# One token block's gate cells: scattered by accumulating indirect transfers in place of one-hot products

## The reference, cut to what matters

```
q = h @ w_q                                    # 8 heads, two halves of 128
s1, s2 = q_half @ sub_keys_{1,2}.T             # 128 scores each
v1, i1 = top_k(s1, 16);  v2, i2 = top_k(s2, 16)
best, ci = top_k(v1[:, None] + v2[None, :], 16)   # 16 pairs of 256, per head
expert = i1[ci // 16] * 128 + i2[ci % 16]
gate = softmax(best)
a = gelu(h . U[expert]) * gate                 # 128 experts a token
out = sum over the 128 of a * V[expert]
```

## Time and profile before

| | |
|---|---|
| median of 3 runs | 2063.12 us (2060.56 to 2063.41) |
| the profiled execution | 2064.9 us, of which the span is 2063.1 us |
| TensorE busy | 2032.0 us, 98% |
| VectorE busy | 1641.9 us, 80% |
| ScalarE busy | 893.3 us, 43% |
| GpSimd busy | 383.9 us, 19% |
| moved by DMA | 471.40 MB, 228 GB/s over the span |

### The profile page before, as it was taken

One profiled execution on the slowest core, in us unless ns is written; L12 is line 12 of the kernel. 1 busy time (PEld: TensorE's weight loads), 2 busy tenths in 40 slices (PEclk: granted clock), 3 DMA queues, 4 the chain that ended last, 5 costly groups with the idle time before them and its releaser, 6 DMA issues.

```text
span 2063.1 us, 28548 instructions
## 1 busy us (share of the span) xinstructions
PE 2032.0 (98%) x10753; PEld 1763.9 (85%) x10753; DVE 1641.9 (80%) x3092; ACT 893.3 (43%) x1369; POOL 383.9 (19%) x297
## 2 busy tenths in 40 slices
PE   8999999999999999999999999999999999999998
PEld 6877788887887788889999999999998888888886
DVE  5787567666986545899999999888668888888887
ACT  5566454544245423534344444444334333333334
POOL 2000110000000001000221222222223444444440
PEclk9999989999999999999999999999999999999999
DMA  7511145531221132224879989999999999999993
GB/s 252 174 51 43 51 161 192 183 143 62 92 82 72 62 102 87 80 82 136 273 263 306 343 285 333 341 319 347 360 355 402 359 376 372 376 370 369 373 375 137
DMA packets 136856, 471.40 MB, mean 228 GB/s; under 512 B 10048, under 2 KB 59456, under 8 KB 110992
## 3 DMA queue, kind: packets, MB, share of 16 engines
q1 hardware_dynamic: 49936, 309.33, 41.2%
q0 software_dynamic: 36864, 134.23, 16.7%
q10 hardware_dynamic: 49920, 26.01, 4.3%
HBM read 416.97 MB, written 52.43 MB: 228 GB/s over the span
## 4 chain that ended last, share of the span: by engine, by line
PE 39%; DVE 10%; issue 1%; ACT 0%
PE bank L158 38%; DVE whl L311 2%; DVE row L2332 2%; DVE room L2276 1%; DVE fg L2283 1%; DVE room L2272 0%; DVE room L2200 0%; DVE cst L2200 0%; DVE y_tok L2200 0%; DVE room L2204 0%; DVE y_tok L2204 0%; DVE cst L2204 0%; DVE cidx L1988 0%; DVE wk L1982 0%; DVE cidx L1980 0%
## 5 line engine op out<-in xcount | busy, mean ns | idle before, releaser
L158 PE MATMUL bank<-xhl,whl 128*128 128x384 f32 (+1 forms) x5256 | 1073.4, 361 | 16.1 <-DVE whl L543 8.2
L158 PEld LDWEIGHTS bank<-xhl,whl 128*128 128x128 f32 x5256 | 935.7, 188 | 103.1 <-issue 10.2
L311 DVE TENSOR_TENSOR whl<-raw,whl 128x1024 fp32r<-128x1024 f32 (+2 forms) x397 | 472.6, 1201 | 198.9 <-ACT whl L304 152.5
L158 PE MATMUL bank<-whl,ag 128*128 128x512 f32 x2304 | 526.3, 390 | 0.8 <-issue 0.8
L158 PEld LDWEIGHTS bank<-whl,ag 128*128 128x128 f32 x2304 | 431.4, 188 | 91.5 <-ACT whl L304 2.0
L304 ACT ACTIVATE whl<-raw 128x1024 fp32r<-128x1024 f32 (+2 forms) x397 | 398.8, 1024 | 86.7 <-PE bank L158 78.6
L2319 POOL DMA_INDIRECT row<-in_U_rows,row_at x128 | 149.5, 1168 | 597.9 <-DVE row L2332 429.8
L2319 POOL DMA_INDIRECT row<-in_V_rows,row_at x128 | 191.0, 1492 | 251.3 <-DVE y_tok L2348 221.8
L2348 DVE SCALAR_TENSOR_TENSOR y_tok<-row,row_a,y_tok 128x1024 f32<-128x1024 f32 x127 | 162.6, 1280 | 2.6
L2332 DVE SCALAR_TENSOR_TENSOR row<-row,h_tok 128x1024 f32<-128x1024 f32 x128 | 155.7, 1218 | 0.1
L158 PE MATMUL bank<-yhl,whl 128*128 128x512 f32 x636 | 150.8, 392 | 1.6 <-DVE whl L311 1.0
(11 more groups left out here) (286 smaller groups left out, 1763.9 us busy)
## 6 DMA issues: line engine op xcount, KB each, us to landing
raw<-in_U SPq DMA_DIRECT2D x64, 1024.0 KB, 7.5
raw<-in_V SPq DMA_DIRECT2D x64, 1024.0 KB, 6.8
hidden<-h_both SPq DMA_DIRECT2D x32, 768.0 KB, 10.4
gates<-g_stage ACTq DMA_DIRECT2D x12, 2048.0 KB, 21.7
g_ring<-gates SPq DMA_DIRECT2D x32, 768.0 KB, 10.9
h_ring<-hidden SPq DMA_DIRECT2D x22, 768.0 KB, 8.2
raw<-in_w_ada SPq DMA_DIRECT2D x16, 1024.0 KB, 5.7
raw<-in_w_gla SPq DMA_DIRECT2D x12, 1024.0 KB, 4.9
```

The lines of the kernel that those rows point to most:

```text
L158: return e.matmul(o, a, b, start=start, stop=stop, skip_group_check=True)
L311: e.tensor_tensor(lo[:, s], src[:, s], F(hi[:, s]), ALU.subtract).then_inc(dve_lo.of((i, half)))
```

## The change

The gates of block 0 (`THROWN`) are no more spread by one-hot rows. Their places in `gates` are filled with zeros early, from the zero halves of `kz`: 16 transfers of 512 KB on SP's queue, two behind each of the loads 12 to 19. When block 0 is chosen, six more operations of 128x128 or less on VectorE work out the place of each of its 128 x 128 gates in `gates` (`cell`), and GpSimd adds them in by 128 indirect transfers with an add (`throw`), each of 128 elements of 4 bytes, one for each partition. They stand in pairs ahead of the gathers 24 to 87. Two heads of a token may choose the same expert, so the first of the 16 transfers of a head waits until the last head's have landed. Blocks 1 and 2 (`TURNED`) are spread as before: 64 spreads in place of 96, 8 stores in place of 12, and 6 transposes in place of 9. `in_turn` is changed too: block 1 is chosen alone in slots 25.5 to 43.5, block 2 with a spread at each second step in slots 43.5 to 67.5, and the other spreads follow at four in three slots up to slot 100. The load of the first group of the V stage waits for the thrown gates too.

```
+THROWN = (0,)
+TURNED = tuple(qt for qt in BLOCKS if qt < ND and qt not in THROWN)
...
         def sync_mla(e, q):
-            load_ahead(e, q, 12, 19)
+            q.wait_ge(act_l0["kpe", 1])
+            for i in range(12, 20):
+                load_ahead(e, q, i, i)
+                for qt in THROWN:
+                    for n in range(2):
+                        a, g = slice(64 * n, 64 * n + 64), slice(4 * (i - 12), 4 * (i - 12) + 4)
+                        e.dma_start(gates[g, a, qt * T:(qt + 1) * T].rearrange("g a x -> a g x"),
+                                    F(KZ[1 - n][a]).unsqueeze(1).broadcast_to([64, 4, T])
+                                    ).then_inc(put_zeros.of((qt, i, n)), 16)
...
-        SPREADS = range(0, TD, 4)
+        SPREADS = [t0 for qt in TURNED for t0 in range(qt * P, (qt + 1) * P, 4)]
+        STORES = len(SPREADS) * 4 // CT
...
-            for _ in range(2 * CHOICE):
+            for n in range(3 * CHOICE // 2):
+                if n % 3 < 2:
+                    next(choose)
+                yield
+            for _ in range(CHOICE):
                 next(choose)
                 yield
                 next(spread)
                 yield
-            for n in range(3 * (len(SPREADS) + 3 - 2 * CHOICE) // 2 + 1):
+            for n in range(3 * (len(SPREADS) + 3 - CHOICE) // 2 + 1):
...
-                        if n == at and qt < ND:
+                        if n == at and qt in TURNED:
...
+                elif qt in THROWN:
+                    q.wait_ge(dve_u["second", qt])
+                    e.tensor_copy(bits_u[:, 0:P], fg).then_inc(dve_u.of(("whole", qt)))
+                    q.wait_ge(dve_u["whole", qt])
+                    e.tensor_scalar(bits_u[:, 0:P], bits_u[:, 0:P], 3, None, ALU.bitwise_and).then_inc(dve_u.of(("in group", qt)))
+                    q.wait_ge(dve_u["in group", qt])
+                    e.tensor_copy(bits[:, P:2 * P], bits_u[:, 0:P]).then_inc(dve_u.of(("lane", qt)))
+                    e.tensor_scalar(fg, fg, float(P * TD), C("cell")[:, qt:qt + 1], ALU.mult, ALU.add
+                                    ).then_inc(dve_u.of(("group", qt)))
+                    q.wait_ge(dve_u["lane", qt], dve_u["group", qt])
+                    e.scalar_tensor_tensor(fg, bits[:, P:2 * P], float(CT - P * TD), fg, ALU.mult, ALU.add
+                                           ).then_inc(dve_u.of(("second cell", qt)))
+                    q.wait_ge(dve_u["second cell", qt])
+                    e.scalar_tensor_tensor(cell[qt], f_row, float(4 * TD), fg, ALU.mult, ALU.add).then_inc(dve_u.of(("cell", qt)))
...
         def pool_rows(e, q):
 
+            def throw(qt, h, k):
+                if h + k == 0:
+                    q.wait_ge(dve_u["cell", qt], dve_u["gate", qt], put_zeros.all())
+                if h > 0 and k == 0:
+                    q.wait_ge(put_thrown[qt][(h - 1) % 2][h - 1, 15])
+                j = 16 * h + k
+                e.indirect_dma_start(every_gate, bass.IndirectOffsetOnAxis(cell[qt][:, j:j + 1], 0), thrown[qt][:, j:j + 1], None,
+                                     compute_op=ALU.add).then_inc(put_thrown[qt][h % 2].of((h, k)), 16)
+
             q.wait_ge(dve_u["row at"])
             for n in range(2 * P):
+                if 24 <= n < 24 + P // 2:
+                    for j in (2 * (n - 24), 2 * (n - 24) + 1):
+                        throw(0, j // 16, j % 16)
                 if n >= RROW:
                     q.wait_ge(dve_row[n - RROW])
...
                 if g == NG - 2:
-                    q.wait_ge(pe_u["one-hot", TD - 4], dve_u["one-hot", TD - 4], act_u["gates", TD - 4],
-                              *[put_gates[i][TD // CT - 2 + i] for i in range(2)])
+                    q.wait_ge(pe_u["one-hot", SPREADS[-1]], dve_u["one-hot", SPREADS[-1]], act_u["gates", SPREADS[-1]],
+                              *[put_gates[i][STORES - 2 + i] for i in range(2)],
+                              *[s.all() for qt in THROWN for s in put_thrown[qt]])
```

More of the change, by code:

```diff
@@ L46 @@
 CONST = {"ident": (0, 128), "ones": (128, 128), "iota": (256, 128), "rel": (384, 512),
-         "reset": (896, 512), "starts": (1408, 16)}
-NCONST = 1424
+         "reset": (896, 512), "starts": (1408, 16), "cell": (1424, 3)}
+NCONST = 1427
 PLAN = ([("l0_in", i, ITEM) for i in range(7)]
@@ L246, in build @@
         put_gates = [sig(f"put_gates{i}", 16) for i in range(2)]
+        put_zeros = sig("put_zeros", 16)
+        put_thrown = {qt: [sig(f"put_thrown{qt}_{i}", 16) for i in range(2)] for qt in THROWN}
         put_hidden = [sig(f"put_hidden{i}", 16) for i in range(2)]
@@ L1227, in scalar_gla @@
         def scalar_gla(e, q):
+            q.wait_ge(put_zeros.all())
             split_hi(e, q, IT["w_gla", 0], (1,))
@@ L1293, in vector_gla @@
         def vector_gla(e, q):
-            q.wait_ge(in_rel["rel"])
+            q.wait_ge(in_rel["rel"], put_zeros.all())
             def first(h):
@@ L2125, in pe_spread @@
             yield
-            for t0 in SPREADS:
+            for m, t0 in enumerate(SPREADS):
                 b = u_banks.fill(q, ("gates", t0))
@@ L2129, in pe_spread @@
                 for j in range(4):
-                    oh = one_hot[t0 // 4 % 3]
+                    oh = one_hot[m % 3]
                     for part in range(2):
-                        m = mul(e, b[:, j * P:(j + 1) * P], oh[:, 0, j // 2, 0, :, j % 2], oh[:, 1, j // 2, part, :, j % 2],
-                                j + part == 0)
-                m.then_inc(pe_u.of(("one-hot", t0)))
+                        last = mul(e, b[:, j * P:(j + 1) * P], oh[:, 0, j // 2, 0, :, j % 2],
+                                   oh[:, 1, j // 2, part, :, j % 2], j + part == 0)
+                last.then_inc(pe_u.of(("one-hot", t0)))
                 u_banks.give(("gates", t0), (act_u, ("gates", t0)))
@@ L2172, in leave @@
                     e.dma_start(gates[:, :, ch * 4 * CT:(ch + 1) * 4 * CT].rearrange("g a x -> a g x"),
-                                stage.rearrange("p (g x) -> p g x", g=NG)).then_inc(put_gates[ch % 2].of(ch), 16)
+                                stage.rearrange("p (g x) -> p g x", g=NG)).then_inc(put_gates[c % 2].of(c), 16)
             yield
-            for t0 in SPREADS:
-                if t0 >= 8:
-                    leave(t0 - 8)
+            for m in range(len(SPREADS)):
+                if m >= 2:
+                    leave(m - 2)
                 yield
-            for t0 in SPREADS[-2:]:
-                leave(t0)
+            for m in (len(SPREADS) - 2, len(SPREADS) - 1):
+                leave(m)
                 yield
@@ L2265, in dve_choose @@
                                                                 ("second", bits, iota[:, 0:16], ALU.is_equal))):
-                    dst = f_row if qt == ND and s == 0 else fg
+                    dst = f_row if qt not in TURNED and s == 0 else fg
                     for part in range(4):
@@ L2343, in dve_rows @@
                 if n == 0:
-                    q.wait_ge(pe_u["one-hot", TD - 4])
+                    q.wait_ge(pe_u["one-hot", SPREADS[-1]])
                     e.tensor_scalar(y_tok, t, a, None, ALU.mult).then_inc(dve_row.of(P + n))
@@ L2776, in layouts @@
     consts[:, 1408:1424] = [0, 16, 32] + [48 + 4 * j for j in range(13)]
+    for qt in range(ND):
+        consts[:, 1424 + qt] = (4 * qt + i // CT) * (4 * CT) + i % CT
     r["consts"] = consts
```

51 lines of the change are left out of this document (30 added, 21 removed).

## The result

| | median of runs | profiled run | its span | granted clock |
|---|---|---|---|---|
| before | 2063.3 us (2060.6 to 2064.6, 4 runs) | 2064.9 | 2063.1 | 0.996 |
| after | 2123.2 us (2120.7 to 2129.1, 4 runs) | 2122.2 | 2120.5 | 0.985 |

After takes 1.0298 times before's time, with a 95% interval of 1.0285 to 1.0312: 60 us slower. The forecast was 2044 us and faster; of the times on record the measured one is nearest to rival B's, on the other side (2104 us, a throw costs more to issue than a gather).

A forecast was written before the change was run, and what follows sets the result against it. The prediction took TensorE to bound the kernel, busy for 98% of the span: 2064.9 - 17.6 (spreads) - 1.5 (transposes) = 2045.8 us profiled, 1.8 less for the median, so 2044 us; likeliest case 2038 to 2052, full range 2038 to 2125.

The forecast's parts named there:

- rival B: On GpSimd, a throw costs more to issue than a gather, 1.98 us: 2104 us in all; chance 0.26.
- The spreads and transposes: On TensorE, 32 spreads by 0.55 us and three transposes taken out save 19.1 us.
- The zeros: 16 issues on SP's queue, 8.4 MB, hidden by slack ahead of the weights: cost taken as 0.
- The window of 64 slots: U stage slots 36 to 100, where the throws stand: 306.6 us before, 304 us predicted after.
- the throw's price: On GpSimd, issue and gap of one throw, taken from a gather's median: 1.45 us, between 1.24 and 2.27.
- GpSimd's need: GpSimd's time in the window for 192 issues at 1.45 us and seven waits: 310 us against 304.
- seven waits: GpSimd waits for the last head's throws to land, 6 us less 1.45 for a gather between: 32 us.
- The break-even price: On GpSimd, the time per issue at which all of the 19 us gain is gone: 1.59 us.
- the cover: Gathers issued four slots ahead leave 8.7 us, VectorE's lead 5.2: 14 us of GpSimd's excess not reaching TensorE.
- rival A: GpSimd's issues meet VectorE at any phase, 1.56 us each; 13 us reach TensorE: 2057 us; chance 0.16.
- Rival C: Thrown elements are slow in the DMA engines, 150 ns each, deciding from 45 ns: 2167 us; chance 0.11.
- D: No change, as VectorE's pace in slots 43.5 to 67.5 or a late store keeps TensorE's gain: 2063 us; chance 0.05.

The follow-up runs named there:

- no_throws: The changed kernel without its 128 throws, block 0's gates staying zero, the rest of the change kept: 2042.1 us, 0.9897 of before.
- no_add: The changed kernel with throws that write their elements in place of adding them: 2052.6 us.
- gaps: The changed kernel with each head's 16 throws within ten gathers, then one or two gathers free, 11.5 gathers to a head: 2055.9 us, 0.9975 of before.
- issue_twice: The changed kernel with throws that write in place of adding, and two GpSimd fills of a spare tile ahead of each throw: 2120.3 us.
- wide: The changed kernel with the throws spread at thirteen gathers to a head, up to gather 113: 2071.4 us, 1.0037 of before.
- the spread kernels: Variants of the changed kernel with the throws spread over more gathers than 24 to 87, in various spacings: 2045.2 to 2071.4 us.
- front_wide: The changed kernel with the throws spread at thirteen gathers for each of three heads, eleven for the other five: 2054.8 us, 0.9966 of before.
- the two kernels with the spare tile: The changed kernel with writing throws, and one or two GpSimd fills of a spare tile ahead of each: 2073.8 and 2120.3 us.

## Why the prediction was wrong

**Right.** The spreads and transposes: 19.1 us predicted, 19.7 measured (no_throws). The zeros: no cost to be seen. A slot not held up still takes 4.16 us. The window of 64 slots, 304 us in the sum, is 1390.20 - 1086.96 = 303.2 in no_throws. The load of the first group stands at 1544.24 in after, 65 us behind the last throw; I had said 80.

**The step that failed** is the throw's price in GpSimd's need, "I take 1.45", from a gather's row. It measured 1.706 + 0.30 = 2.01 us. The terms of GpSimd's need:

| | in the sum | measured in after |
|---|---|---|
| 128 throws | 128 x 1.45 = 186 | 218.3 + 36.9 = 255 |
| gathers | 64 x 1.45 = 93 | 81 + 19 = 100 (63) |
| seven waits | 32 | 38.5 |
| need | 310 | 394 |

Of the 84 us that the need is larger, some 70 are the throws'. The break-even price stood in the text, 1.59 for every issue or 1.66 for a throw beside gathers at 1.45, and 2.01 is well past both.

**The stretch and the cover** were a little off too, on two sides. The 394 us run from the first throw to gather 87. In no_throws the same stretch is 295.6 us, since gather 87 starts ahead of the last of the 64 slots: 394.0 - 295.6 is the 98.4 that after is late. With gather 87 counted in and the whole 303.2 us against it, as the sum had it, 395.3 - 303.2 = 92 us are over, and 81 were lost. So the cover in the sum's sense was 11, and 10 to 12 in the other three kernels that were 39 us late or more. I had taken 14.

**What makes an issue dear.** Part of the step was wrong even for a plain write: no_add's is 1.27 + 0.30 = 1.57, which is rival A's 1.56, and A's place (10 us lost) held. The add's own share is no_add's difference (1.56 against 0.97 at least); the rest depends on VectorE. In after a throw of 2.54 us began at 1104.99, beside two operations of VectorE of 1.22 us from 1104.88 and 1106.02; it ended at 1107.53, 0.3 behind the second. That is no single case: of the 65 throws in no_add that took 0.15 us or more above the least, 61 ended at one of three fixed distances behind an operation of VectorE (figures in the last section). The Trainium skill (SBUF — State Buffer, Who interferes with whom) says that a VectorE instruction with two SBUF inputs contends with a GpSimd instruction that reads SBUF. VectorE's rows and low parts have two SBUF inputs, and the trace agrees in that the issue ends behind VectorE's operation. A throw took 1.71 us in the mean where VectorE was busy for 274.04 of 393.80 us (70%), and 1.83 in gaps, where it was for 350.83 of 426.00 (82%). So a kernel whose GpSimd is less late, and whose VectorE is busier for it, pays more for each issue.

**Rival B** had the mechanism, that an add costs more to issue, and nearly the price (1.98 against 2.01), which it had borrowed from a gather that met VectorE. Its reason, that an add has two things to read, no run shows. It gave 2104 and not 2123, because its need was 378, 16 us short (2 in the throws, 7 in the gathers, 7 in the waits), and its cover 3 too large. The waits in after are 5.5 us each in the mean, 3.3 to 7.3: a head's last throw landed 7.1 us after its issue in the mean (8.3 in the case shown) and not 6.

**Rival C** is out as the cause of this loss: issue_twice lost 68 us with plain writes, and the DMA share in after's stretch was 0.86. Its term was no small one, though. q0 took 18.5% x 2120.5 x 16 - 16.7% x 2063.1 x 16 = 764 us more, 48 us of all sixteen engines or 47 ns an element, in place of my 28; that is at the 46 us from which C was to decide. Within 304 us it might have cost some us of its own, had GpSimd been fast enough; no run here shows that. Spread over a longer stretch it fits: wide has a share of 0.98 between 1085 and 1479 and has lost 3.5 us by then. **D** is out by no_throws, 19.7 us below before.

**What the prediction passed over** came up only with the spread kernels: SP's wait for the last throw, with the weights of V and the stores of hidden queued behind it. In after it costs nothing, 65 us being free; it binds once the throws reach up to gather 108 or 113.

**Open.** The 11 us that front_wide loses behind slot 119 were placed by the waits of its trace; no kernel takes one of these waits away. Open too are a first-group load that doesn't wait at the head of SP's queue, which wasn't tried, why an add is dearer to issue than a write, and the 12 us in the two kernels with the spare tile.

## What to carry to other kernels

Price an indirect transfer that accumulates by its own row, not by a gather's: on the issuing engine it cost 1.71 us in the mean here, a gather before 1.17. Count idle time where the new work will stand: of the 435 us that GpSimd was idle before, some 237 lay in the slots where the throws went. Add up the need of the issuing engine (busy, gap after each issue, waits) for the stretch and set it against the stretch's length; the excess, less a cover of 16 to 18 us, was the loss in four kernels that were over by more than 38 us. When work is spread out to fit, look next at who waits for its last piece, and at what is queued behind that wait.

## What the runs showed of the hardware

- An indirect transfer of 128 elements of 4 bytes: to issue it took GpSimd 1.56 us at least and 1.71 in the mean with an add, 0.97 and 1.27 without; 144 packets against 32 (18432 / 128 and 4096 / 128, from q0 in after, issue_twice and before). With the add there is at least one packet for each of the 128 elements.
- An issue on GpSimd that is slow ends at one of a few fixed distances behind an operation of VectorE: in no_add 61 of the 65 slow throws ended 0.11 to 0.13, 0.23 to 0.26 or 0.84 to 0.86 us behind one, each an operation with two inputs. Points put at random would do so in 9% of cases. A throw grew from 0.97 to as much as 1.97 us by it.
- A scattered transfer of 512 bytes with the add lands late: 7.1 us from the end of its issue in the mean of seven (8.3 in the case shown), nearly as long as a gathered row of 512 KB took before.
- TensorE's granted clock fell with its own waits: 1.00 ahead of the throws, 0.94 in the stretch in which it is busy for 342 of 394 us, and 1.00 in no_throws in the same stretch at 393 of 394. It adds nothing to the loss as accounted here, since GpSimd sets that stretch.
- In the two kernels with a spare SBUF tile of 640 bytes a partition, 2304 products of the V stage took 538.5 us in place of 526.3, at a granted clock of 1.00. The tile was not tried alone.
